# Hybrid RG-LRU and HGRN2 layer: order of the weight pieces in the first loop body, and which engine splits and scales them

## The reference

```python
mod = silu(c) @ ada_w + ada_b                       # 1024 -> 3072
shift, scale, gate = split(mod, 3)
hn = rmsnorm(x, pre_w) * (1 + scale) + shift
xa, ga, q, fr, iv, gb = split(hn @ w_in)            # 1024 -> 6 x 512
xc, conv_new = causal_conv(xa)                      # width 4
h  = rg_lru(xc)                                     # scan, gates by block-diagonal products
ya = h * silu(ga)
f  = lb + (1 - lb) * sigmoid(fr); k = (1 - lb) * sigmoid(-fr)
o, S = hgrn2(q, log(f), k, iv)                      # 4 heads of 128
yb = rmsnorm(o, onorm_w) * silu(gb)
m  = concat(ya, yb) @ w_out                         # 1024 -> 1024
y  = x + gate * rmsnorm(m, post_w)
```

## Time and profile before

| what | value |
| --- | --- |
| runs | 1025.59, 1025.9, 1026.58 us |
| profiled execution, span | 1026.3 us (no other time of it is given) |
| busy: TensorE, VectorE, ScalarE, Pool | 984.2, 582.0, 430.0, 161.0 us |
| granted TensorE clock, mean | 0.981 |
| chain that ended last | TensorE 90%, VectorE 5%, issue 2% |

### The profile page before, as it was taken

The page is one execution under the profiler, slowest core; times in us unless marked ns, Lnnn a source line. Parts: engine busy times, 40 slices in busy tenths (PEclk is TensorE's granted clock), DMA queues, the critical chain, the costliest instruction groups (busy, mean ns, idle before and its releaser), DMA issues.

```text
span 1026.3 us, 19994 instructions
## 1 busy us (share of the span) xinstructions
PE 984.2 (96%) x7423; PEld 714.3 (70%) x7478; DVE 582.0 (57%) x1652; ACT 430.0 (42%) x810; POOL 161.0 (16%) x208
## 2 busy tenths in 40 slices
PE   7899986899999999999999999999999999999987
PEld 3465875469775887579766976697759775887554
DVE  1453688436763576436754566366635773477445
ACT  2531747313651365135713373237413661345321
POOL 4000024301130112011110112011301130111212
PEclk9999998899999999999999999999999999999998
DMA  9984301100110011000110011001101010100413
GB/s 313 326 275 130 118 24 59 62 2 21 42 63 0 20 41 43 19 20 0 42 62 0 21 41 62 0 21 41 62 0 41 0 50 1 42 1 23 118 42 111
DMA packets 46590, 60.62 MB, mean 59 GB/s; under 512 B 2748, under 2 KB 40208, under 8 KB 46524
## 3 DMA queue, kind: packets, MB, share of 16 engines
q1 hardware_dynamic: 46524, 59.86, 17.8%
HBM read 48.90 MB, written 10.95 MB: 58 GB/s over the span
## 4 chain that ended last, share of the span: by engine, by line
PE 90%; DVE 5%; issue 2%; ACT 1%; DMA 1%; SPq 1%; DVEq 0%; ACTq 0%
PE ring L390 66%; PE lev L464 7%; PE aux L507 3%; PE okv L521 2%; PE lev L469 1%; PE okv L491 1%; PE lev L462 1%; PE ring L521 1%; PE okv L493 1%; PE okv L492 1%; DMA work<-in_w_in_dram 1%; PE okv L811 1%; PE aux L441 1%; PE aux L477 1%; PE aux L428 1%
## 5 line engine op out<-in xcount | busy, mean ns | idle before, releaser
L390 PE MATMUL ring<-hnh,wih 128*128 128x256 bf16 (+1 forms) x1152 | 291.1, 264 | 5.8 <-DVE hnl L1273 4.2
L390 PE MATMUL ring<-hnh,wil 128*128 128x256 bf16 (+1 forms) x1152 | 291.2, 264 | 0.0
L390 PE MATMUL ring<-hnl,wih 128*128 128x256 f16 (+1 forms) x1152 | 291.1, 264 | 0.0
L390 PE MATMUL ring<-woh,work 128*128 128x512 f16 x512 | 162.3, 379 | 1.7
L390 PEld LDWEIGHTS ring<-hnh,wih 128*128 128x128 f16 x1152 | 112.5, 100 | 18.1 <-issue 4.5
L1165 DVE TENSOR_TENSOR qq<-qq,gg 128x256 f32<-128x256 f32 x96 | 44.1, 459 | 140.1 <-PE lev L464 99.8
L390 PEld LDWEIGHTS ring<-hnl,wih 128*128 128x128 f16 x1152 | 110.6, 98 | 12.9
L390 PEld LDWEIGHTS ring<-hnh,wil 128*128 128x128 bf16 x1152 | 110.6, 98 | 12.4
L390 PE MATMUL ring<-wih,hnh 128*128 128x512 f16 (+1 forms) x264 | 101.1, 383 | 4.0 <-ACT kk L851 4.0
L390 PE MATMUL ring<-wih,hnl 128*128 128x512 f16 (+1 forms) x264 | 101.1, 383 | 1.4 <-issue 0.2
L1587 POOL TENSOR_TENSOR kk<-kk,cols 128x256 f32<-128x256 f32 x32 | 29.3, 935 | 419.3 <-ACT kk L851 419.3
(11 more groups left out here) (310 smaller groups left out, 1585.5 us busy)
## 6 DMA issues: line engine op xcount, KB each, us to landing
xin<-in_x_prompt_dram SPq DMA_DIRECT2D x16, 512.0 KB, 3.4
work<-in_x_prompt_dram SPq DMA_DIRECT2D x16, 512.0 KB, 4.3
out_dram<-work SPq DMA_DIRECT2D x16, 512.0 KB, 2.6
work<-in_ada_w_dram SPq DMA_DIRECT2D x4, 1024.0 KB, 10.4
woh<-in_ada_w_dram SPq DMA_DIRECT2D x4, 1024.0 KB, 11.8
work<-in_w_in_dram SPq DMA_DIRECT2D x4, 1024.0 KB, 7.2
woh<-in_w_in_dram SPq DMA_DIRECT2D x4, 1024.0 KB, 8.5
wol<-in_w_in_dram SPq DMA_DIRECT2D x4, 1024.0 KB, 9.6
```

The lines of the kernel that those rows point to most:

```text
L390: last = mm(out, a(k), b(k), start=start and k == ks[0] and j == 0, stop=stop and k == ks[-1] and j == 2)
```

## The change

- The order of loads becomes ada 2 to 7, w_in 0 to 11, ada 8 to 11, w_out 0 to 3. The staging places follow from it: w_in 6 to 11 come into places 0 to 5, ada 8 to 11 into 0 to 3.
- The low halves of w_in pieces 5, 7, 9 and 11 are made on Pool (`rest_in`), each with the semaphore `w_lo_pool`, between the forget bounds of the first and of the second pair. VectorE makes 6 after level 3, 8 after level 6 and 10 after the row norms of the first pair. It made 5 after level 0, 6 after level 7, 7 and 8 after the row norms, 9 and 10 after the forget floor and 11 after the first convolution.
- ScalarE copies 6 and 7 behind the second V eviction, 8 and 9 behind the two GB evictions, 10 and 11 around the squares of the next rows.
- `fold` on VectorE is gone. ScalarE multiplies the four lower row tiles of a w_out piece itself, with one copy of 256 columns each, scaled by `onorm_w`, right ahead of its copy into woh.
- TensorE, SP, ScalarE and Pool wait for both semaphores where they waited for `w_lo`.

```diff
--- before.py
+++ after.py
@@ -210,7 +210,7 @@
         ada_ps, mod_sb, mod_ps = sem("ada_ps"), sem("mod_sb"), sem("mod_ps")
         mod_ok, gate_ok, gp_ps, gp_sb = sem("mod_ok"), sem("gate_ok"), sem("gp_ps"), sem("gp_sb")
         w_hi = sem("w_hi")
-        w_lo, wo_lo, w_fold = sem("w_lo"), sem("wo_lo"), sem("w_fold")
+        w_lo, w_lo_pool, wo_lo, w_fold = sem("w_lo"), sem("w_lo_pool"), sem("wo_lo"), sem("w_fold")
 
         d_ld, d_s0 = sem("d_ld"), sem("d_s0")
         chain_dve, chain_pool = sem("chain_dve"), sem("chain_pool")
@@ -232,8 +232,10 @@
 
         NEARLY, NADA, NWI, NWO = 2 * D // 256, 3 * D // 256, PIN // 256, D // 256
         WI_COLS = (FR, Q_, IV, IV + 256, GB, GB + 256, FR + 256, Q_ + 256, XA, GA, XA + 256, GA + 256)
-        pieces = ([("ada", i) for i in range(len(early), NEARLY)] + [("wi", i) for i in range(6)]
-                  + [("ada", i) for i in range(NEARLY, NADA)] + [("wi", i) for i in range(6, NWI)] + [("wo", i) for i in range(NWO)])
+        POOL_LOW = (5, 7, 9, 11)
+        on_pool = [sum(c < i for c in POOL_LOW) for i in range(NWI + 1)]
+        pieces = ([("ada", i) for i in range(len(early), NEARLY)] + [("wi", i) for i in range(NWI)]
+                  + [("ada", i) for i in range(NEARLY, NADA)] + [("wo", i) for i in range(NWO)])
         place, landed, before = {}, {}, {}
         users = [[] for _ in stage]
         for _i, _piece in enumerate(pieces):
@@ -316,8 +318,12 @@
                     pk, pc = before[kind, c]
                     if pk == "ada":
                         sp.wait_ge(ada_ps, pc + 1)
+                    elif pk == "wo":
+                        sp.wait_ge(wo_lo, pc + 1)
+                    elif pc in POOL_LOW:
+                        sp.wait_ge(w_lo_pool, on_pool[pc + 1])
                     else:
-                        sp.wait_ge(*((w_lo, pc + 1) if pk == "wi" else (wo_lo, pc + 1)))
+                        sp.wait_ge(w_lo, pc + 1 - on_pool[pc + 1])
                 src, col = {"ada": (ada_v, 256 * c), "wi": (w_in_v, WI_COLS[c % NWI]), "wo": (w_out_v, 256 * c)}[kind]
                 sp.dma_start(stage[place[kind, c]], src[:, :, col:col + 256]).then_inc(st_ld[place[kind, c]], 16)
                 if i == 6:
@@ -547,8 +553,9 @@
                 def weights(i):
 
                     if first:
-                        pe.wait_ge(w_lo, i)
-
+                        pe.wait_ge(w_lo, i - on_pool[i])
+                        if on_pool[i]:
+                            pe.wait_ge(w_lo_pool, on_pool[i])
 
                 weights(1)
                 if not first:
@@ -945,8 +952,11 @@
                 s = stage[place[kind, c]]
                 act.wait_ge(st_ld[place[kind, c]], landed[kind, c])
                 if kind == "wo":
-                    act.wait_ge(w_fold, c + 1)
-                    act.wait_ge(w_lo, NWI)
+                    for k in range(CT):
+                        A(s[:, CT + k, :], s[:, CT + k, :], ACT.Copy, scale=pcol("onw", k)).then_inc(w_fold, 1)
+                    act.wait_ge(w_fold, CT * (c + 1))
+                    act.wait_ge(w_lo, NWI - len(POOL_LOW))
+                    act.wait_ge(w_lo_pool, len(POOL_LOW))
                 dst, col = (wih, WI_COLS[c]) if kind == "wi" else (woh, 256 * c)
                 A(dst[:, :, col:col + 256], s, ACT.Copy).then_inc(w_hi, 1)
 
@@ -967,15 +977,14 @@
                 for t in range(NT):
                     act.wait_ge(iv_ps.sem, iv_ps.at(n, t + 1))
                     A(vv[:, t, :], ring[t][:, :], ACT.Copy).then_inc(v_sb.sem, 1)
-                    if t == 0:
-                        weights("wi", 5)
+                    weights("wi", *((5,), (6, 7))[t])
                 for t in range(NT):
                     act.wait_ge(gb_ps.sem, gb_ps.at(n, t + 1))
                     A(gbs[:, t, :], ring[t][:, :], ACT.Silu).then_inc(gb_sil.sem, 1)
+                    weights("wi", 8 + t)
                 if not first:
                     squares_m(n - 1, 0)
                 else:
-                    head("wi", 6)
                     mod_out(4, ring[0])
                 k_out(n, 0)
                 squares_o(n, 0)
@@ -984,7 +993,7 @@
                 else:
                     mod_out(5, ring[1])
                 squares_o(n, 1)
-                weights("wi", 7)
+                weights("wi", 10)
                 if not last_body:
                     squares_x(n + 1)
                 else:
@@ -994,17 +1003,15 @@
                             act.wait_ge(dv("xsq_d"), 1)
                         A(junk[0:TD, 0:512], xin[0:TD, 0, 512 * c:512 * c + 512], ACT.Square, accum_out=xssq[0:TD, c:c + 1])\
                             .then_inc(dv("xsq_d"), 1)
-                weights("wi", 8)
+                weights("wi", 11)
                 gate_out(n, 1)
                 q_out(n, 1)
-                weights("wi", 9, 10)
                 if first:
                     act.wait_ge(gp_ps, 1)
                     for i in range(2):
                         last = A(gp[:, 512 * i:512 * i + 512], lev[i][:, :], ACT.Copy)
                     last.then_inc(gp_sb, 1)
                 xa_out(n, 0)
-                weights("wi", 11)
                 ga_out(n, 0)
                 gates_out(n, 0)
                 weights("wo", 0)
@@ -1295,13 +1302,6 @@
                 V.tensor_tensor(hnl[:, :, 0:TD], hx3, hnh[:, :, 0:TD], ALU.subtract).then_inc(dv("hn"), 1)
                 V.tensor_copy(gprow.rearrange("p (k b l) -> p k b l", k=KT, b=NB), seqs(gpt)).then_inc(dv("gprow"), 1)
 
-            def fold(c):
-
-                dve.wait_ge(st_ld[place["wo", c]], landed["wo", c])
-                v = stage[place["wo", c]][:, CT:, :]
-                onw = par[:, ROW["onw"]:ROW["onw"] + CT].unsqueeze(2).to_broadcast([P, CT, 256])
-                V.tensor_tensor(v, v, onw, ALU.mult).then_inc(w_fold, 1)
-
             def body(n, first, last_body):
                 def weights(*which):
                     if first:
@@ -1319,9 +1319,8 @@
                     y_split(n - 1)
                 for l in range(LEVELS + 1):
                     take(n, 0, l)
-                    if l == 0:
-                        weights(5)
-                weights(6)
+                    if l in (3, 6):
+                        weights(4 + 2 * l // 3)
                 if not first:
                     m_out(n - 1, 0)
                 state(n, 0, 0)
@@ -1329,7 +1328,7 @@
                     m_out(n - 1, 1)
                 state(n, 0, 1)
                 rows(n, 0)
-                weights(7, 8)
+                weights(10)
                 if first:
                     dve.wait_ge(mod_ps, 6)
                     gate = aux[0][:, 0:KT * NS].rearrange("p (k s) -> p k s", s=NS)
@@ -1338,15 +1337,10 @@
                 else:
                     x_out(n - 1, 0)
                 forget(n, 1)
-                weights(9, 10)
                 take(n, 1, 0)
                 conv(n, 0)
-                weights(11)
                 take(n, 1, 1)
                 take(n, 1, 2)
-                if first:
-                    fold(0)
-                    fold(1)
                 if not last_body:
                     x_norm(n + 1)
                 else:
@@ -1370,9 +1364,7 @@
                     hn_rest(n + 1, 1)
                     hn_rest(n + 1, 2)
                     hn_rest(n + 1, 3)
-                if first:
-                    fold(2)
-                else:
+                if not first:
                     m_out(n - 1, 2)
                 state(n, 1, 0)
                 if not first:
@@ -1380,9 +1372,7 @@
                 state(n, 1, 1)
                 rows(n, 1)
                 input_scale(n, 1)
-                if first:
-                    fold(3)
-                else:
+                if not first:
                     x_out(n - 1, 1)
 
             chain = [0]
@@ -1622,15 +1612,24 @@
             def rest(c):
 
                 cols = slice(256 * c, 256 * c + 256)
-                pool.wait_ge(w_lo, NWI)
+                pool.wait_ge(w_lo, NWI - len(POOL_LOW))
                 pool.wait_ge(w_hi, NWI + c + 1)
                 G.tensor_tensor(wol[:, :, cols], stage[place["wo", c]], woh[:, :, cols], ALU.subtract).then_inc(wo_lo, 1)
 
+            def rest_in(c):
+
+                cols = slice(WI_COLS[c], WI_COLS[c] + 256)
+                pool.wait_ge(w_hi, c + 1)
+                G.tensor_tensor(wil[:, :, cols], stage[place["wi", c]], wih[:, :, cols], ALU.subtract).then_inc(w_lo_pool, 1)
+
             def body(n, first):
                 bounds(n, 0)
                 if not first:
                     h_save(n - 1, 1)
                     y_head(n - 1)
+                else:
+                    for c in POOL_LOW:
+                        rest_in(c)
                 halo_in(n, 0)
                 bounds(n, 1)
                 halo_save(n, 0)
```

## The result

| kernel | median us (runs) | ratio to the kernel before, 95% interval |
| --- | --- | --- |
| before | 1026.21 (20) | 1 |
| changed | 1028.16 (20) | 1.0018 [1.0011, 1.0026] |
| changed, on another occasion | 1027.78 (12) | 1.0011 [1.0001, 1.0021] |
| before against itself | 1025.77 (12) | 0.9990 [0.9981, 1.0000] |

Each ratio is to runs of the kernel before on the same occasion (median 1027.24 us for the third row, 1026.61 us for the fourth), so the medians of different rows are not compared. The change makes the kernel slower by one to two microseconds. The forecast was 1.9 us more, 1027.8 us. The kernel before against itself came out 1 us faster, so a single comparison here is not read finer than that.

What follows compares the result with a forecast made beforehand. TensorE sets the pace to about 140 us, then a ScalarE, Pool and VectorE chain up to the second body's gate sigmoid. First half 4.9 us later, second 6.5 back, chain from 1.6 early to 1.9 late: 1027.8 us, range 1023.0 to 1031.0.

Steps and rivals of the forecast that it cites:

- First half: First body up to about the key turn: Pool's low halves of w_in make TensorE 4.9 us later.
- Level 4: First head pair: TensorE idles 1.9 us before this level because Pool's piece 7 holds the level 3 update.
- The first gate-column product: First ada product in ring[0]: its load lands at 86.8, wanted at 87.8, so cost 0.
- the clock: Behind TensorE's waits in the first body: an idle time of 1.4 us or more costs 1.7 us on top.
- Second half: Later part of the first body: waits of 1.4 and 1.7 us and their clock losses go, 6.5 us back.
- Both waits: TensorE's 1.4 us for a low half of w_in and 1.7 us before a level go, each with 1.7 us of clock.
- The chain: Input sigmoid to the second body's gate sigmoid: ScalarE's scaling, 1.7 us a piece, turns 1.6 us early into 1.9 late.
- rival 3: Input scale slips in ahead of Pool's w_out subtraction: up to 3.8 us go, 1024.0 us; chance 0.10.
- Its own signs of being wrong: Levels 2 and 4 on time, TensorE waiting for a DMA, or the kk L851 wait ending before 186.4.
- rival 1: Pool's pieces fall between VectorE's operations without delaying levels: the 4.9 us go, 1022.9 us; chance 0.15.
- rival 2: Gate columns come late at the first ada product in ring[0]: 1030.3 to about 1034.8 us; chance 0.20.
- Rival 4: Clock does not fall after the new 1.9 us wait, or waits are smaller: -1.7, 1026.1 us; chance 0.13.

Runs made afterwards that it cites:

- first profile of the kernel before: The kernel before, unchanged, as first profiled: span 1026.3 us, belonging to a run of about 1028.05 us, 2 us above its median.
- median profile: The kernel before, run and profiled once more with no edit: 1025.95 us, near its median of 1025.77, with a span of 1024.2 us.

## Why the prediction was right, step by step

**First half, said to cost 4.9 us.** It costs 3.1 us: the forget projection of the second pair starts at 105.01 us, against 101.95 in the first profile of the kernel before, which starts the V projection at the same 57.41. By parts: level 2 started at 70.10 against 69.50, 0.6 us late as said. Level 4 started after 1.60 us, said 1.9. The key turn was due 0.7 us late and had no wait. The first gate-column product waited 0.36 us for its load, said 0: the load landed about when it was said to, at 86.6 against 86.8, but TensorE wanted it at 86.26 and not at 87.8. The term that was mis-sized is the clock, and it explains that earlier arrival too: 1.7 us were added behind the wait before level 4, and in this execution there were none.

```profile
79.80:82.30 2.50, 2.45 (x13) 1.18 (x13) 2.50 (x5) 0.00 (x0) 0.00 (x0) 1.00 0.00 0
```

I had taken two cases of a fall behind waits of 1.4 and 1.7 us for a rule. The kernel before run again shows one of the same two without it. Nor is the new wait free of it: in the profile of the kernel with the scaling back on VectorE, which has this half unchanged, the same wait of 1.60 us is followed by a fall. Its levels 4 and 5 start at 79.11 and 84.31, 5.20 us apart and not 3.50, at a clock of 0.67 between them. So the 1.7 us forecast do come in some executions; how often is not shown.

**Second half, said to give back 6.5 us.** Both waits went as said. From the forget projection to the gates of the first pair TensorE takes 134.49 - 105.01 = 29.5 us; in the first profile of before it took 138.17 - 101.95 = 36.2 us, so 6.7 us. Against the median profile, which lacks one of the two falls, it is 34.6 - 29.5 = 5.1 us.

**The chain, said to lose 3.5 us** (from 1.6 us early to 1.9 us late). From the input sigmoid to the gate sigmoid of the second body, changed against first profile of before:

```profile
136.47 0.84 ACT L915 ACTIVATE ii<-aux,par 128x256 f32<-128x256 f32 x2
137.20 1.70 ACT L956 ACTIVATE work<-work,par 128x256 f32<-128x256 f32 x4
...
145.34 4.30 DVE L1246 SCALAR_TENSOR_TENSOR rr<-xc,rr 128x512 f32<-128x512 f32 x1
...
174.71 4.45 DVE L1246 SCALAR_TENSOR_TENSOR rr<-xc,rr 128x512 f32<-128x512 f32 x1
...
181.92 1.91 ACT L961 ACTIVATE woh<-work 128x2048 f16<-128x2048 f32 x1
```

The input sigmoid is 3.68 us early (136.47 against 140.15), the copy of piece 3 only 0.10 us (181.92 against 182.02). 3.6 us are lost between, 3.5 were worked out (3.3 by the median profile), and 1.70 us is the price of a piece's scaling. The input scale was caught beside Pool both times, as said; rival 3 did not happen.

**The sum.** By the profiled executions the change is 4.9 - 3.1 = 1.8 us better than forecast: 1.9 forecast, 0.1 measured. By the medians it is 1.9 us. Both are explained by the base. I took the profile of before for a run like its median, 0.4 us apart; it was one of 2 us more, since its own time is its span plus 1.75 us. From the V projection of the first body to the start of the sigmoid of k in the second, the median profile of before has 184.68 - 57.79 = 126.9 us and the changed kernel 185.63 - 57.41 = 128.2 us, 1.3 us more. Behind it the clock costs more. These are the start of the V projection and of the first level of the second body, with the same 24 products between them, in the median profile of before and in the changed kernel:

```profile
185.33 0.39 PE L390 MATMUL ring<-wih,hnh 128*128 128x512 f16 x1 [4.02 <-ACT kk L851]
...
192.21 1.05 PE L462 MATMUL lev<-qq,kk 128*128 128x128 f32 x8
```

```profile
186.28 0.61 PE L396 MATMUL ring<-wih,hnh 128*128 128x512 f16 x1 [5.10 <-ACT kk L858]
...
194.30 1.05 PE L468 MATMUL lev<-qq,kk 128*128 128x128 f32 x8
```

That is 6.88 us in the kernel before, behind 4.0 us of idle time, and 8.02 us in the changed one behind 5.1 us: 1.1 us more, where the forecast had put nothing. 1.3 + 1.1 is 2.4 to 2.5 us. The median profile starts the V projection of the first body 0.4 us later than the changed kernel, which leaves the 2.1 us that lie between the starts of these two levels, and 2.2 us lie between the spans. So the mechanism of each step stood, and the sizes of the clock's terms were wrong: against the median profile the first half cost 1.8 us less than said, the second gave back 1.4 us less, and 1.1 us came behind the gate wait. These errors cancelled, and that is the luck in the number. That the longer fall comes from the longer wait is not shown: two profiles of the changed kernel with equal waits have 8.02 and 7.30 us there, and two of the kernel before have 7.75 and 6.88.

**Its own signs of being wrong.** Two of them came. TensorE did wait for a load (0.36 us), and the wait for the sigmoid of k ended at 186.28 us, before the 186.4 that was set; 188.2 was expected. The first is the clock term again, as above. The second was set from a profile that was no typical one: against the median profile the wait ends 1.3 us later, counted from the V projection of the first body.

**The rivals.** Pool's pieces did delay the levels (rival 1 is out, by the rows above and the run with all of them on VectorE). The gate columns were late by 0.36 us, and the clock stayed at 1.00 behind it, so rival 2 came only in its smallest form. (Its price for a landing time of 7 us has a slip: the load of piece 10 would land at 98.4, 1.5 us after 96.9 and not 1.8.) Rival 4, the clock does not fall behind the new wait, did happen in both profiled executions of the changed kernel, and yet its 1026.1 us did not, because the errors above made up for it.

## What to carry to other kernels

Moving work to an idle Pool is not free for VectorE where both read SBUF: count the time of Pool's instruction on VectorE too, at its own 4.07 us and not at VectorE's 2.29, and look first at the Pool work that is already there. In the kernel before, the four w_out subtractions on Pool, which the change left there, cost 6 us, against 1 to 2 us for the change itself. And before a sum is set against a median, ask whether the profile is of a median run; one clock fall more or less was as large as the whole effect.

## What was not expected of the hardware

TensorE's clock falls in some executions and not in others behind the same wait. Behind the 1.7 us before a level it was 0.58 in one profile of the kernel before and 1.00 in the other, over the same 4.1 us. Behind the 1.4 us for a low half it was 0.75 in both, and 1.00 in the kernel with the w_out halves on VectorE, which has the same wait of 1.42 us there (its profiled execution, 1017.9 us, was its fastest, 2.5 us below its median):

```profile
109.00:114.30 5.30, 5.30 (x49) 4.77 (x50) 3.11 (x3) 3.08 (x4) 2.12 (x4) 1.00 0.21 59
```

Behind the new wait of 1.6 us in the changed kernel none is seen in either of the two profiles taken: levels 4 and 5 start 3.50 us apart in both (78.80 and 82.30, 78.81 and 82.31), near the 3.43 us of the kernel before. Behind the same wait in the kernel with the scaling back on VectorE they start 5.20 us apart (79.11 and 84.31). What decides it is not shown.
